# Handing two 512 KB round trips through memory from the sync queue to ScalarE's queue

## The chip, the cores and the metric

One core of a Trainium2 chip runs the whole kernel. The metric is the device time of one execution in microseconds (us); the time that is quoted is the median of several executions.

## What is computed

One layer of a hybrid encoder on 256 tokens of width 2048, in float32. Cut to what matters here:

```
u = rmsnorm(x) @ W_in
x = x + concat(fox_attention(u), ssd(u)) @ W_out          # the "output" groups o0..o3
g, up = split(rmsnorm(x) @ W_gate_up)
x = x + (silu(causal_dwconv3(g)) * up) @ W_down           # the "down" groups, 0..3
x = x + sigmoid(rmsnorm(x) @ W_ple_gate) * (p @ W_ple_proj)
out = rmsnorm(x)
```

## The kernel before

**Chunks.** Every product with a weight is made by streaming the weight in chunks of 128 x 1024 float32 (512 KB). A chunk is loaded by the sync queue (SP) into one of four slots of `w_raw`, split by ScalarE (ACT) into `w_hi` (`make_hi`, L349) and by VectorE (DVE) into the rest, `w_lo` (`make_lo`, L354), and used by TensorE (PE) in 12 matmuls, high times high, high times low and low times high. Four chunks are in the ring: the load of chunk n waits for `w_lo` of chunk n-4, and `make_hi` of chunk n waits until PE has used chunk n-4. So when ACT makes chunk 3 of a section, PE has just ended the last chunk of the section before.

**The turning.** The residual x lies in `xtok` with tokens on the partitions. The next product needs it with features on the partitions, split into a high and a low part (`hHi`, `hLo`, both in the tile `h_parts`). For each group of 512 output columns this is done in steps:
- DVE adds the group's PSUM banks to `xtok` (`add_columns`, L1499) and transposes blocks of 32 x 32 into `turn_blocks` (L1538).
- `carry_out` (L460): one DMA of 512 KB writes these blocks to `turn_dram` in HBM.
- `carry_back` (L471): when it has landed, four DMAs of 128 KB read them back in pieces of 512 bytes into `turned_cols`, with features on the partitions.
- `turn_out` or `turn_down`: ACT makes four tiles of 128 x 256 of the high part (L1128), DVE four of the low part (L1489).

ACT meanwhile squares the new columns (`square_columns`, L1146) and, when the group is the last of its product, takes the root for the norm (`root_x`, L1155). The norm's factor is applied later, so that nothing here waits for it but the root itself.

**The order.** Each engine runs its instructions in the order in which they are written, and that order is set by hand: the number k (or n) of the chunk behind which a step stands. `LEAD` is 3 and `KU` is 8. A section "gate_up, first half" has 8 chunks, and chunk k of it multiplies features 2k and 2k+1 (blocks of 128), so that chunk 6 is the first that needs the blocks 12 and 13 of the last output group o3. In the last section ("tail") the first gate group has the order gate chunks 0 to 5, one chunk of `W_ple_proj` (place 6), gate chunks 6 and 7: the blocks 12 and 13 of the last down group are needed at place 7.

The last group of each product stands apart from the others: its `carry_out` is written behind place `LAST_OUT` of the chunks that follow and its `carry_back` behind `LAST_BACK`; `LAST_H` = 8 is the place at which ACT and DVE make the blocks. A queue that runs the step first waits: `carry_out` for `blocks_made` and for the landing of the group before, `carry_back` for the landing of the write (`blocks_out`) and for `h_lo_made`, which says that `turned_cols` has been read for the group before.

Of the kernel before, what the change touches and what calls it, by code (L numbers as in the profile page):

```python
# [46 lines left out]
def build(nc, x, p, mix_norm_w, w_in, fox_forget_bias, ssd_conv_w, ssd_conv_b, ssd_dt_bias, ssd_A_log,  # L47
          ssd_D, ssd_norm_w, w_out, ffn_norm_w, w_gate_up, ffn_conv_w, ffn_conv_b, w_down, ple_norm_w,
          w_ple_gate, w_ple_proj, final_norm_w, out):
    _, T, D = x.shape  # L50
    TT = T // P
    KD = D // P
# [17 lines left out]
    KU = KD // 2  # L70
# [34 lines left out]
    NDN = D // COLS  # L105
# [23 lines left out]
    with ctx:  # L129
# [189 lines left out]
        def load_chunk(sp, n, src, q=0):  # L319
            if n >= RING:  # L320
                sp.wait_ge(w_lo_made, n + RING * q - RING + 1)
            sp.dma_start(w_raw[:, n % RING, :].rearrange("p (a c) -> p a c", a=src.shape[1]), src).then_inc(w_landed[n % RING], 16)

        def load_unit_chunk(sp, n, src, q=0):
            if n >= RING:
                sp.wait_ge(w_lo_made, n + RING * q - RING + 1)
            for a in range(2):
                sp.dma_start(w_raw[:, n % RING, a * COLS:(a + 1) * COLS].rearrange("p (b c) -> p b c", b=2),
                             src[:, a, :, :]).then_inc(w_landed[n % RING], 16)
# [13 lines left out]
        def make_hi(act, n, q=0):  # L343
            act.wait_ge(*landed(n, q))
            if RING <= n < n_last:
                act.wait_ge(w_used, n + RING * q - RING + 1)
            elif n >= n_last + KP - 1:
                act.wait_ge(w_used, n_last)
            act.activation(parts(n)[0], w_raw[:, n % RING, :], ACT.Copy).then_inc(w_hi_made, 1)  # L349
# [6 lines left out]
        def chunk_of(g, c):  # L356
            return g.view[:, 2 * c:2 * c + 2, g.col:g.col + COLS]
# [88 lines left out]
        def carried_before(norm, i):  # L446
            return NDN * (norm - 1) + i
# [6 lines left out]
        def carry_out(sp, norm, i):  # L454

            n = carried_before(norm, i)
            sp.wait_ge(blocks_made, TT * (n + 1))
            if n > 0:
                sp.wait_ge(cols_landed, 64 * n)
            sp.dma_start(turn_dram.rearrange("t p c -> p t c"), turn_blocks[norm - 1][:, :, :]).then_inc(blocks_out, 16)  # L460

        def carry_back(sp, norm, i):

            n = carried_before(norm, i)
            sp.wait_ge(blocks_out, 16 * (n + 1))
            if i > 0:
                sp.wait_ge(h_lo_made, norm * KD + MT * i)
            by_quarter = turn_dram.rearrange("t (i k) (j c) -> j k (t i) c", k=BLK, j=NB)
            for j in range(NB):
                rows_ = slice(j * BLK, (j + 1) * BLK)  # L470
                sp.dma_start(turned_cols[norm - 1][rows_, :, :, :].rearrange("p a m q -> p a (m q)"),  # L471
                             by_quarter[j]).then_inc(cols_landed, 16)
# [47 lines left out]

        LEAD = 3
        CARRY_OUT, CARRY_BACK, H_AFTER = LEAD + 5, LEAD + 7, LEAD + 7
        LAST_OUT, LAST_BACK, LAST_H = LEAD + 5, LEAD + 6, LEAD + 5
        assert LAST_H == KU
        GROUP_OUT, GROUP_BACK, GROUP_READY, Z0_LATER = LEAD + 5, LEAD + 6, LEAD + 6, 3
        end = {g.name: done[g.name] for g in in_groups + out_groups}
# [94 lines left out]
        def run(table, n, steps):  # L621
            for name, args in table.get(n, ()):
                if name in steps:
                    steps[name](*args)
# [15 lines left out]
        def _(sp):  # L640
# [44 lines left out]
            for j in range(2):  # L685
                for k in range(KU):
                    run(sp_before, n_ffn + j * KU + k, steps)
                    if j * KU + k == LAST_OUT:
                        carry_out(sp, 1, NDN - 1)
                    if j * KU + k == LAST_BACK:  # L690
                        carry_back(sp, 1, NDN - 1)
                    load_unit_chunk(sp, n_ffn + j * KU + k, gu[:, 2 * k:2 * k + 2, :, j * 2 * P:(j + 1) * 2 * P])
            with sp.Fori(0, NU // 2 - 1) as i:
                for j in range(2):
# [26 lines left out]
                    for j in range(RING):  # L721
                        load_chunk(sp, n0 + peeled + j, wdn_v[:, bass.ds(q * (2 * RING) + 2 * (peeled + j), 2), cols], q)
            for i, (g, c) in enumerate(tail):
                if i == LAST_OUT:
                    carry_out(sp, 2, NDN - 1)
                if i == LAST_BACK:
                    carry_back(sp, 2, NDN - 1)
                load_chunk(sp, n_ple + i, chunk_of(g, c))
                if i == RING:

                    sp.dma_start(gain_fin[:, :], final_norm_w.rearrange("(a n) -> a n", a=1).to_broadcast([P, D])).then_inc(gain_fin_landed, 16)
# [394 lines left out]
        def _(act):  # L1126
# [22 lines left out]
            def root_x(norm):  # L1149
                if norm == 0:  # L1150
                    act.wait_ge(x_squared, TT)
                    act.wait_ge(tables_loaded, 1)
                else:
                    act.wait_ge(x_summed, norm)
                act.activation(root[:, :], x_sum[:, norm, :], ACT.Sqrt, bias=eps[:, :], scale=1.0 / D).then_inc(root_made, 1)  # L1155
# [136 lines left out]
            def leave_out(i):  # L1292
                square_columns(1, i)

            def turn_out(i):
                for k in range(MT * i, MT * (i + 1)):
                    make_h(1, k, par_ffn)

            def leave_down(g):
                square_columns(2, g)  # L1300

            def turn_down(g):
                for k in range(MT * g, MT * (g + 1)):
                    make_h(2, k, par_ple)
# [27 lines left out]
            def unit_leave(u, half, unit_end):  # L1332

                act.wait_ge(w_used, unit_end)
                act.wait_ge(rms_col_made, 2)
                if not (isinstance(u, int) and u == 0):
                    act.wait_ge(unit_turned, u * TT)
                for t in range(TT):
                    copy(unit_tok[:, t, :], ps[:, UNIT_BANKS[half][t], :], rms_col[:, t:t + 1]).then_inc(unit_left, 1)
# [18 lines left out]
            for j in range(2):  # L1358
                for k in range(KU):
                    make_hi(act, n_ffn + j * KU + k)  # L1360
                    if j == 0:
                        run(act_after, n_ffn + k, steps)
                        if k == LEAD:
                            leave_out(NDN - 1)
                        if k == LEAD + 1:
                            root_x(1)
                    else:
                        if k == 0:
                            turn_out(NDN - 1)
                        if k == U_LEAVE:  # L1370
                            unit_leave(0, 0, n_ffn + KU)
# [27 lines left out]
            def ple_sigmoid(i, only=(0, 1)):  # L1399
                for t in only:  # L1400
                    if t == 0:
                        act.wait_ge(gate_first, i + 1)
                        act.wait_ge(rms_col_made, 3)
                    else:
                        act.wait_ge(w_used, n_ple + GROUP * (i + 1) if i < NDN - 1 else n_last + 1)
                    if i > 0:
                        act.wait_ge(ple_mul, TT * (i - 1) + t + 1)
                    act.activation(pg_sig[:, t, :], ps[:, GATE_BANKS[i % 2][t], :], ACT.Sigmoid,
                                   scale=rms_col[:, t:t + 1]).then_inc(ple_sig, 1)

            def square(i, t):
                act.wait_ge(out_added, TT * i + t + 1)
                if i + t > 0:
                    act.wait_ge(out_squared, TT * i + t)
                act.activation(squares[:, :], xtok[:, t, i * COLS:(i + 1) * COLS], ACT.Square,
                               accum_out=out_ssq[:, t, i:i + 1]).then_inc(out_squared, 1)

            for n in range(len(tail)):
                make_hi(act, n_ple + n)
                if n == LEAD:  # L1420
                    leave_down(NDN - 1)
                if n == LEAD + 1:
                    root_x(2)
                if n == LAST_H:
                    turn_down(NDN - 1)
                for i in range(NDN - 1):
                    if n == i * GROUP + SIG_AT:
                        ple_sigmoid(i)
                    if n == i * GROUP + SQUARE_AT:
                        for t in range(TT):  # L1430
                            square(i, t)
# [576 lines left out]
```

## Time and profile before

| | |
|---|---|
| time, median of 3 runs | 1205.61 us (1204.74 to 1206.5) |
| the profiled execution's own time | 1207.3 us |
| its span | 1205.4 us |
| TensorE busy | 1192.6 us, 99% of the span |
| VectorE busy | 794.1 us |
| ScalarE busy | 674.1 us |
| mean granted clock of TensorE | 0.998 of full speed |

The span runs from the first to the last instruction of the profiled execution; the 1.9 us between it and that execution's time lie around it. All places in the trace are in us from the span's start. A busy PE is an engine with a matmul in it.

### The profile page before, as it was taken

How to read it: one execution, taken by the hardware profiler on the slowest of the kernel's cores; microseconds unless marked ns; L12 is line 12 of the kernel's file. 1: busy time of each engine (PE TensorE's matmuls, PEld its weight loads, DVE VectorE, ACT ScalarE, POOL GpSimd, SP SyncE). 2: the span in 40 equal slices, each digit the busy share in tenths (PEclk: the TensorE clock that was granted, in tenths of full speed). 3: DMA queues.
4: the chain of work that ended last, by engine and by line, in shares of the span. 5: the costliest groups of instructions: out<-in, count | busy, mean ns of one | idle time of the engine just before them, and what ended most of it. 6: DMA issues, size and time to landing. Idle time of an engine off the chain costs nothing.

```text
span 1205.4 us, 16744 instructions
## 1 busy us (share of the span) xinstructions
PE 1192.6 (99%) x5444; PEld 987.6 (82%) x5444; DVE 794.1 (66%) x1211; ACT 674.1 (56%) x901; POOL 35.3 (3%) x55
## 2 busy tenths in 40 slices
PE   9999999999999999999999999999999999999997
PEld 6888888888888788888888888888888888888886
DVE  5688787886667576766766767667655555555655
ACT  6555787676546555555645655555444444445555
POOL 3210110000100000000000000000000000000000
PEclk9999999999999999999999999999999999999999
DMA  8767996449677877777787787877867676767662
GB/s 276 219 200 241 282 279 191 125 136 261 204 229 248 258 235 244 239 246 241 228 252 242 238 248 229 249 246 231 246 205 220 204 224 198 216 210 248 206 193 105
DMA packets 227511, 270.96 MB, mean 225 GB/s; under 512 B 23136, under 2 KB 152388, under 8 KB 227332
## 3 DMA queue, kind: packets, MB, share of 16 engines
q1 hardware_dynamic: 225972, 266.57, 71.2%
q0 software_dynamic: 1312, 3.47, 1.0%
q8 instruction: 29, 0.48, 0.2%
q10 hardware_dynamic: 176, 0.27, 0.1%
q14 instruction: 22, 0.18, 0.0%
HBM read 247.66 MB, written 22.59 MB: 224 GB/s over the span
## 4 chain that ended last, share of the span: by engine, by line
PE 97%; DMA 1%; ACT 1%; DVE 0%; issue 0%; SPq 0%; ACTq 0%
PE ps L1054 13%; PE ps L1055 13%; PE ps L1056 13%; PE ps L485 11%; PE ps L487 11%; PE ps L486 11%; PE ps L1091 7%; PE ps L1089 7%; PE ps L1090 7%; PE ps L365 2%; DMA turn_dram<-turn_blocks 1%; PE ps L983 1%; PE ps L998 0%; PE ps L961 0%; PE ps L948 0%; PE ps L857 0%
## 5 line engine op out<-in xcount | busy, mean ns | idle before, releaser
L354 DVE TENSOR_TENSOR w_lo<-w_raw,w_hi 128x1024 fp32r<-128x1024 f32 x412 | 502.4, 1222 | 344.4 <-ACT w_hi L349 343.3
L349 ACT ACTIVATE w_hi<-w_raw 128x1024 fp32r<-128x1024 f32 x412 | 434.8, 1058 | 418.3 <-PE ps L1056 201.9
L1054 PE MATMUL ps<-w_hi,h_parts 128*128 128x512 f32 x704 | 274.0, 389 | 2.3 <-DVE h_parts L1489 2.3
L1055 PE MATMUL ps<-w_lo,h_parts 128*128 128x512 f32 x704 | 273.9, 389 | 0.0
L1056 PE MATMUL ps<-w_hi,h_parts 128*128 128x512 f32 x704 | 273.9, 389 | 0.0
L485 PE MATMUL ps<-w_hi,h_parts 128*128 128x512 f32 (+1 forms) x428 | 170.0, 397 | 0.0
L487 PE MATMUL ps<-w_hi,h_parts 128*128 128x512 f32 (+1 forms) x428 | 166.1, 388 | 0.0
L486 PE MATMUL ps<-w_lo,h_parts 128*128 128x512 f32 (+1 forms) x428 | 166.0, 388 | 0.0
L1054 PEld LDWEIGHTS ps<-w_hi,h_parts 128*128 128x128 f32 x704 | 132.2, 188 | 30.3 <-DVE h_parts L1489 2.7
L1056 PEld LDWEIGHTS ps<-w_hi,h_parts 128*128 128x128 f32 x704 | 132.2, 188 | 27.3
L1055 PEld LDWEIGHTS ps<-w_lo,h_parts 128*128 128x128 f32 x704 | 132.2, 188 | 27.3
L1089 PE MATMUL ps<-w_hi,act_parts 128*128 128x512 f32 x352 | 136.9, 389 | 0.0
L1090 PE MATMUL ps<-w_lo,act_parts 128*128 128x512 f32 x352 | 136.9, 389 | 0.0
L1091 PE MATMUL ps<-w_hi,act_parts 128*128 128x512 f32 x352 | 136.9, 389 | 0.0
L487 PEld LDWEIGHTS ps<-w_hi,h_parts 128*128 128x128 f32 x428 | 80.4, 188 | 17.0
L485 PEld LDWEIGHTS ps<-w_hi,h_parts 128*128 128x128 f32 x428 | 80.4, 188 | 15.6
L486 PEld LDWEIGHTS ps<-w_lo,h_parts 128*128 128x128 f32 x428 | 80.5, 188 | 15.4
L1090 PEld LDWEIGHTS ps<-w_lo,act_parts 128*128 128x128 f32 x352 | 66.1, 188 | 13.8
L1091 PEld LDWEIGHTS ps<-w_hi,act_parts 128*128 128x128 f32 x352 | 66.1, 188 | 13.8
L1089 PEld LDWEIGHTS ps<-w_hi,act_parts 128*128 128x128 f32 x352 | 66.1, 188 | 13.5
L485 PE MATMUL ps<-w_hi,mixHi 128*128 128x512 f32 x128 | 50.0, 391 | 0.0
L487 PE MATMUL ps<-w_hi,mixLo 128*128 128x512 f32 x128 | 49.8, 389 | 0.0
(243 smaller groups left out, 1001.2 us busy)
## 6 DMA issues: line engine op xcount, KB each, us to landing
w_raw<-in_w_gate_up SPq DMA_DIRECT2D x352, 256.0 KB, 3.5
w_raw<-in_w_down SPq DMA_DIRECT2D x88, 512.0 KB, 4.3
w_raw<-in_w_in SPq DMA_DIRECT2D x87, 512.0 KB, 4.5
w_raw<-in_w_out SPq DMA_DIRECT2D x32, 512.0 KB, 4.6
w_raw<-in_w_ple_gate SPq DMA_DIRECT2D x32, 512.0 KB, 4.3
unit_cols<-unit_dram SPq DMA_DIRECT2D x88, 128.0 KB, 2.9
unit_dram<-first_blocks SPq DMA_DIRECT2D x22, 256.0 KB, 3.2
unit_dram<-unit_spare SPq DMA_DIRECT2D x22, 256.0 KB, 3.4
```

Of the source, the lines that this page charges most:

```text
L349: act.activation(parts(n)[0], w_raw[:, n % RING, :], ACT.Copy).then_inc(w_hi_made, 1)
L354: dve.tensor_tensor(lo, w_raw[:, n % RING, :], hi, ALU.subtract).then_inc(w_lo_made, 1)
L365: mm = pe.matmul(ps[:, banks[t], :], h_part[:, k, t * P:(t + 1) * P], parts_[:, n % RING, kk * COLS:(kk + 1) * COLS], start=k == 0 and par ...
L485: pe.matmul(dst, a, hi, start=first and kk == 0, stop=False)
L486: pe.matmul(dst, a, lo, start=False, stop=False)
L487: mm = pe.matmul(dst, b, hi, start=False, stop=last and kk == 1)
L1054: pe.matmul(dst, a, hi, start=first and kk == 0, stop=False)
L1055: pe.matmul(dst, a, lo, start=False, stop=False)
L1056: mm = pe.matmul(dst, b, hi, start=False, stop=last and kk == 1)
L1089: pe.matmul(dst, a, hi, start=first and kk == 0, stop=False)
L1090: pe.matmul(dst, a, lo, start=False, stop=False)
L1091: mm = pe.matmul(dst, b, hi, start=False, stop=last and kk == 1)
```

## The change

Both DMA steps of the last output group and of the last down group are taken out of SP's program and written into ACT's, at new places. On SP a place stands ahead of the load of that chunk; on ACT it stands behind `make_hi` of that chunk. In both ACT programs the place `LAST_OUT` falls right behind `root_x`.

```
-        LAST_OUT, LAST_BACK, LAST_H = LEAD + 5, LEAD + 6, LEAD + 5
+        LAST_OUT, LAST_BACK, LAST_H = LEAD + 1, LEAD + 3, LEAD + 5
...
                     run(sp_before, n_ffn + j * KU + k, steps)
-                    if j * KU + k == LAST_OUT:
-                        carry_out(sp, 1, NDN - 1)
-                    if j * KU + k == LAST_BACK:
-                        carry_back(sp, 1, NDN - 1)
                     load_unit_chunk(sp, n_ffn + j * KU + k, gu[:, 2 * k:2 * k + 2, :, j * 2 * P:(j + 1) * 2 * P])
...
             for i, (g, c) in enumerate(tail):
-                if i == LAST_OUT:
-                    carry_out(sp, 2, NDN - 1)
-                if i == LAST_BACK:
-                    carry_back(sp, 2, NDN - 1)
                 load_chunk(sp, n_ple + i, chunk_of(g, c))
...
                         if k == LEAD + 1:
                             root_x(1)
+                        if k == LAST_OUT:
+                            carry_out(act, 1, NDN - 1)
+                        if k == LAST_BACK:
+                            carry_back(act, 1, NDN - 1)
...
                 if n == LEAD + 1:
                     root_x(2)
+                if n == LAST_OUT:
+                    carry_out(act, 2, NDN - 1)
+                if n == LAST_BACK:
+                    carry_back(act, 2, NDN - 1)
```

The sync queue at the start of gate_up, before and then after. Two gate_up loads make one chunk. The first `turned_cols` row is the group o2, the second is o3.

```order
L471 DMA turned_cols_88<-turn_dram 32x8x128 x4
L328 DMA w_raw<-in_w_gate_up 128x2x256 x6
L460 DMA turn_dram<-turn_blocks_87 128x2x512
L328 DMA w_raw<-in_w_gate_up 128x2x256 x2
L471 DMA turned_cols_88<-turn_dram 32x8x128 x4
L328 DMA w_raw<-in_w_gate_up 128x2x256 x14
L693 UNCONDITIONAL_BRANCH
```

```order
L471 DMA turned_cols_88<-turn_dram 32x8x128 x4
L328 DMA w_raw<-in_w_gate_up 128x2x256 x22
L689 UNCONDITIONAL_BRANCH
```

The five DMAs of o3 have left the queue: nothing stands between the loads of chunks 5 to 15 any more.

ScalarE at the start of the tail, before and then after; the one row `w_hi` between the squares (`unit_tok,x_ssq`) and the root is chunk 4.

```order
L1146 ACTIVATE unit_tok,x_ssq<-xtok 128x512 x2
L349 ACTIVATE w_hi<-w_raw 128x1024
L1155 ACT_TABLE_LOAD
L1155 ACTIVATE root<-x_sum,eps 128x2
L349 ACTIVATE w_hi<-w_raw 128x1024 x4
L1128 ACTIVATE h_parts<-turned_cols_90,par 128x256 x4
```

```order
L1138 ACTIVATE unit_tok,x_ssq<-xtok 128x512 x2
L349 ACTIVATE w_hi<-w_raw 128x1024
L1147 ACT_TABLE_LOAD
L1147 ACTIVATE root<-x_sum,eps 128x2
L460 DMA turn_dram<-turn_blocks_89 128x2x512
L349 ACTIVATE w_hi<-w_raw 128x1024 x2
L471 DMA turned_cols_90<-turn_dram 32x8x128 x4
```

The write stands behind the root and ahead of chunk 5, the four reads stand behind chunk 6 and ahead of chunks 7 and 8 and of the making of the blocks. At the start of gate_up ScalarE's rows read the same way, with the four tiles of group o2 between chunks 5 and 6.

## Rows read from the trace of the kernel before

**Rows 1.** The page, part 1: busy time and share of each engine.
```profile
PE 1192.6 (99%) x5444; PEld 987.6 (82%) x5444; DVE 794.1 (66%) x1211; ACT 674.1 (56%) x901; POOL 35.3 (3%) x55
```

**Rows 2.** Waits of TensorE: us in total, times, longest.
```profile
PE ps L1054 <- DVE h_parts L1489: 2.3, 1, 2.3
PE ps L839 <- DVE idle_in L1775: 1.3, 1, 1.3
PE ps L845 <- DMA mix_rows<-in_mix_norm_w: 0.7, 1, 0.7
```

**Rows 3.** Chain that ended last, 377 to 398: start, us, what.
```profile
381.56 1.31 DVE turn_blocks L1538 x2
382.87 0.02 issue
382.88 7.92 DMA turn_dram<-turn_blocks
390.80 0.02 issue
390.82 0.31 SPq L471
...
392.16 2.58 DMA turned_cols<-turn_dram
394.73 0.02 issue
394.76 0.03 ACT h_parts L1128
...
395.70 0.89 DVE h_parts L1489 x2
396.59 0.04 issue
396.63 0.50 PE ps L1054
```

**Rows 4.** Landings of the three earlier writes of turn_blocks (348.0, 359.2, 370.3).
```profile
DMA to landing us min/median/max: 3.1/3.1/3.1
...
DMA to landing us min/median/max: 5.0/5.0/5.0
...
DMA to landing us min/median/max: 5.9/5.9/5.9
```

**Rows 5.** ScalarE in order of time, 384 to 393.
```profile
384.94 0.29 ACT L1155 ACTIVATE root<-x_sum,eps 128x2 f32<-128x2 f32 x1 [1.36 <-DVE x_sum L1512]
385.14 1.04 ACT L349 ACTIVATE w_hi<-w_raw 128x1024 fp32r<-128x1024 f32 x1
...
387.69 1.04 ACT L349 ACTIVATE w_hi<-w_raw 128x1024 fp32r<-128x1024 f32 x1
...
392.08 1.06 ACT L349 ACTIVATE w_hi<-w_raw 128x1024 fp32r<-128x1024 f32 x1 [1.45 <-DMA w_raw<-in_w_gate_up]
```

**Rows 6.** The store that ScalarE's queue issues at the end.
```profile
L1479 ACTq DMA_DIRECT2D out_x<-xtok x1: 367/367/367, 1201.4 to 1201.4; - x1
```

**Rows 7.** VectorE in order of time: the low parts of group o2.
```profile
387.36 1.67 DVE L1489 SCALAR_TENSOR_TENSOR h_parts<-turned_cols,par,h_parts 128x256 fp32r<-128x256 f32 x4
```

**Rows 8.** Sync queue in order of time, 384 to 393.
```profile
384.86 1.21 SPq L328 DMA_DIRECT2D w_raw<-in_w_gate_up  x2
390.82 1.79 SPq L471 DMA_DIRECT2D turned_cols<-turn_dram  x4
```

**Rows 9.** DMA issues, 385.43 to 385.46: the second load of chunk 8.
```profile
w_raw<-in_w_gate_up SPq DMA_DIRECT2D x1, 256.0 KB, 6.6
```

**Rows 10.** Busy time by stretch; the last two columns are DMA share and GB/s.
```profile
384.00:388.00 4.00, 4.00 (x19) 3.34 (x18) 2.85 (x6) 3.06 (x7) 0.00 (x0) 1.00 0.95 324
388.00:392.00 4.00, 4.00 (x20) 3.30 (x19) 3.38 (x5) 1.79 (x2) 0.00 (x0) 1.00 0.22 75
```

**Rows 11.** ScalarE in the tail, in order of time.
```profile
1105.59 0.29 ACT L1155 ACTIVATE root<-x_sum,eps 128x2 f32<-128x2 f32 x1
1105.79 2.21 ACT L349 ACTIVATE w_hi<-w_raw 128x1024 fp32r<-128x1024 f32 x2
...
1113.35 1.69 ACT L1128 ACTIVATE h_parts<-turned_cols,par 128x256 fp32r<-128x256 f32 x4
```

**Rows 12.** Sync queue in the tail, in order of time.
```profile
1103.53 0.37 SPq L460 DMA_DIRECT2D turn_dram<-turn_blocks  x1
...
1106.87 1.81 SPq L471 DMA_DIRECT2D turned_cols<-turn_dram  x4
```

**Rows 13.** DMA issues of the tail: the write at 1103.53; the fourth read, at 1108.2.
```profile
turn_dram<-turn_blocks SPq DMA_DIRECT2D x1, 512.0 KB, 3.3
...
turned_cols<-turn_dram SPq DMA_DIRECT2D x1, 128.0 KB, 4.4
```

**Rows 14.** TensorE in the tail: first matmul of place 7.
```profile
1117.56 0.39 PE L485 MATMUL ps<-w_hi,h_parts 128*128 128x512 f32 x1
```

## The prediction

> **What bounds the kernel now.** The page's busy times come first: TensorE is busy 1192.6 us, 99% of the span [rows 1]. So the change can only be worth what TensorE waits for, and the view of waits says how much that is: 2.3 us once for `h_parts`, and else only waits in the first microseconds [rows 2]. The third view, the chain that ended last, shows that the 2.3 us belong to the very step that is moved. From 382.88 the chain leaves the engines: the write of o3's blocks takes 7.92 us to land, the four reads are issued at 390.82, the last one at 392.16 lands 2.58 us later, ACT makes two tiles from 394.76, DVE ends their low parts at 396.59, TensorE resumes at 396.63 [rows 3]. With no wait it would have resumed at 396.63 - 2.3 = 394.3. The same step in the tail is not on the chain: ACT makes the blocks from 1113.35, 1.87 us later (as 394.76 to 396.63) they could be used at 1115.2, and place 7 starts at 1117.56 [rows 11, 14]. It has 2.3 us to spare.
>
> Why is the write slow? The same 512 KB took 3.1, 5.0, 5.9 and then 7.92 us in the four output groups [rows 3, 4], and 3.3 us in the tail [rows 13]. From 384 to 388 the DMA engines are 0.95 busy [rows 10]: the write stands in SP's queue behind six loads of 256 KB. So its price is mostly a backlog, not the transfer.
>
> **The change, start of gate_up.** Nothing is computed less; the five DMAs only get other start times. I follow them in order.
>
> The write. Now it is issued when the blocks are made, 382.88. After the change ACT issues it behind the root, which ends at 384.94 + 0.29 = 385.23 [rows 5]: 2.35 us later. A DMA issued by ACT costs it 0.37 us [rows 6].
>
> How long it then takes on the other queue no row shows. From below 3.1 us, the calm write [rows 4]. From above: in the kernel before, everything that is posted by 385.44 (the loads of chunks 5 to 7, this write and chunk 8) has landed when the second load of chunk 8 has, 385.44 + 6.6 = 392.04 [rows 9]; a write that came last of all would land there, 6.8 us after its issue. I take 4.6, the middle of the calm tail's 3.3 and o2's 5.9, since its own queue is empty but the engines are not: it lands at 389.85.
>
> The row says that in one queue a backlog costs this write up to 7.92 - 3.1 = 4.8 us. The Trainium skill, DMA: Bandwidth & Descriptors, "Queues, rings and completion order", says that a DMA engine takes turns between the queues for which it has work; by it the write would pass the backlog at about half rate, close to my 4.6. The same page, "Issuing engines are not separate DMA queues", says that issuing from several engines saves only the time of issuing. By that sentence the write would come out near the upper bound, 392.04, and it speaks against this change. No row here has a busy SP queue and an ACT queue side by side, so both stay open.
>
> The reads. ACT reaches them behind chunk 6. Its `make_hi` starts at 387.69 for 1.04 us [rows 5]; with the issue ahead of it (0.37) that ends at 389.1. It also waits for o2's low parts, which end at 387.36 + 1.67 = 389.03 and shift by as much: 389.4 [rows 7]. So the reads begin at B = the later of 389.45 and the landing; by my value 389.85, against 390.82 before. The gain in B is 0.97 us, and never over 1.37.
>
> What is queued behind them. The four issues take 1.79 us on SP [rows 8]; that is now ACT's time. `make_hi` of chunks 7 and 8 follow, one in about 1.0 us: chunk 8 ends at B + 3.8. DVE follows with 1.2 us each and ends `w_lo` of chunk 8 at B + 5.3, then the two low parts, 0.89 [rows 3]: TensorE could not resume before B + 6.1. Before, SP issued them and ACT did chunk 7 meanwhile. The other bound is the landing: before, the last read landed 394.74 - 390.82 = 3.92 us after the first was issued [rows 3]. But then the DMA engines were only 0.22 busy [rows 10], since SP itself, waiting for the write, held back the loads of chunks 9 and 10. After the change these loads go out at about 387.5 and 390.5, and the reads meet the second. In the tail, beside loads, the last read landed 1108.2 + 4.4 - 1106.87 = 5.7 us after the first was issued [rows 12, 13]. I take 4.5, nearer to the row of the place itself, so TensorE resumes at B + 4.5 + 1.87 = B + 6.4, which is over the floor of B + 6.1.
>
> Sum: 389.85 + 6.4 = 396.25, against 396.63: 0.4 us gained. The corners: B = 389.45 and the floor of 6.1 give 395.55, 1.1 us gained; B = 392.04 and 5.7 + 1.87 = 7.6 give 399.6, 3.0 us lost.
>
> The loads that SP issues earlier are worth nothing: hi of chunk 8 did wait for its load until 392.08 [rows 5], but it is needed by TensorE two chunks after chunk 6, and the load moves little, since the same bytes are ahead of it.
>
> **The change, tail.** The root ends at 1105.88 instead of a write issued at 1103.53 [rows 11, 12]: 2.35 us later again, and ACT's order is the same. The write took 3.3 us here [rows 13] and the engines carry less, so B = 1109.2; chunks 5 and 6 end at 1105.79 + 2.21 + 0.37 = 1108.4 and hide under it. The reads land at 1109.2 + 5.7 = 1114.9, the blocks are ready 1.87 us later, 1116.8, and place 7 starts at 1117.56. Cost 0, covered by 0.8 us of gate and projection matmuls. It was 2.3 us, so most of this cover is used up: each microsecond by which the write takes longer than 4.1 comes out of TensorE's time.
>
> In all -0.4 us: 1207.3 - 0.4 = 1206.9 for an execution like the profiled one. The median of the runs is 1.7 us under the profiled one's time, so 1205.61 - 0.4 = 1205.2.
>
> **The rivals.**
> - A, the write doesn't pass the backlog and ACT stands in wait for it. For it: the loads of chunk 8, posted at that very time, took up to 6.6 us [rows 9]. Against it: another queue. ACT's chunks 7 and 8, the tiles and all of DVE hang behind it. B = 392.04 and reads beside loads give +3.0 us, 1208.6. It costs over 2.4 us from B = 391.5 on if the reads take 5.7 us, from 392.9 on if only the order of ACT and DVE counts. 1 in 10.
> - B, milder: write 5 to 6 us, reads 4.5 to 5.7. Break-even is B = 390.2, a write of 5.0 us. The stall grows by 0 to 2.4 us; in the middle +1.1, 1206.7. 18 in 100.
> - C, the cover in the tail is gone: a write of 5.9 us there gives B = 1111.8, blocks ready at 1119.4, a new wait of 1.8 us, 1207.0 with the gain of 0.4. Against it: the calm 3.3. With a bad start of gate_up it makes the run slower. 5 in 100.
> - D, the whole stall goes and more with it, over 2.4 us: 1203.2. Against it: ACT can't issue the reads before 389.45, so 1.1 us is the most that this place gives. 4 in 100.
>
> **How the numbers follow.** The forecast, 0 to 1.1 us gained, has 63 in 100; its own range is 1204.3 to 1206.0. 0.2% is 2.4 us, about what a measurement of this kernel tells from no change. The forecast, B and half of C fall within it: 0.63 + 0.18 + 0.03 = 0.84; faster is D, 0.04; slower is A and the rest of C, 0.12. The three runs before lie 0.9 us to either side of their median, so the low end is 1205.61 - 1.1 - 0.7 = 1203.8, and the high end reaches into A, 1208.0.
>
> **What would show it.** Of the changed kernel: the write issued by ACT's queue at about 385.3, landing near 389.9 (4 to 5 us); the reads issued by ACT within half a microsecond of that; TensorE's wait for `h_parts` between 1.2 and 2.3 us and still the only one past the start; ACT's `make_hi` of chunk 7 about 2 us later than before; in the tail no wait of TensorE. I am wrong if the write lands after 391 (A, B), if the reads take over 5 us from the first issue, if a wait stands at 1117, or if TensorE's wait is under 1.2 us, which would say that ACT's order is no floor.

## The result, and the profile after

The changed kernel takes 1212.93 us (median of 6 runs, 1211.65 to 1215.11), the kernel before 1205.5 us (6 runs, 1204.74 to 1207.57). The ratio is 1.0059 with a 95% interval of 1.0049 to 1.0068: 7.4 us slower. The prediction was 1205.2 us, in a range of 1203.8 to 1208.0. In the runs of this document two executions fell into a much slower state, one of e4 (2137.47 us) and one of the kernel before beside e8 and e10 (1719.88 us); no ratio contains them, the medians as given do.

The profiled execution of the changed kernel took 1211.92 us, with a span of 1210.2 us, 4.8 us over the span before. In the order of the prediction, first the waits of TensorE (us in total, times, longest us):

```profile
PE ps L1046 <- DVE h_parts L1489: 4.0, 1, 4.0
PE ps L485 <- DVE h_parts L1489: 1.6, 1, 1.6
PE ps L831 <- DVE idle_in L1775: 1.3, 1, 1.3
```

The wait at gate_up is 4.0 us and not 2.3 [rows 2], and there is a new one of 1.6 us, L485, in the tail. Together 3.3 us more. The rest shows only in the busy time by stretch; its columns are those of [rows 10], and the number after POOL is the granted clock:

```profile
392.00:396.00 4.00, 0.66 (x3) 0.20 (x2) 1.69 (x3) 1.22 (x4) 0.00 (x0) 1.00 1.03 302
396.00:402.00 6.00, 5.34 (x13) 4.18 (x14) 2.62 (x5) 1.44 (x3) 0.00 (x0) 0.50 0.51 161
402.00:404.00 2.00, 2.00 (x9) 1.58 (x8) 0.67 (x1) 1.06 (x1) 0.00 (x0) 0.79 0.02 7
```

TensorE had been idle since 392.66. From 396 to 402 its granted clock is 0.50, the lower of its two levels (1.2 and not 2.4 GHz), and 0.79 as the mean of 402 to 404 is another 0.84 us of it: 6.8 us in all. The chain that ended last shows the same, and the path to it (start us, us, what):

```profile
383.26 4.73 DMA turn_dram<-turn_blocks
388.01 0.34 ACTq L471
...
389.38 5.38 DMA turned_cols<-turn_dram
...
396.66 0.79 PE ps L1046
397.45 0.43 PE ps L1047
397.88 0.43 PE ps L1048
...
403.23 0.23 PE ps L1046
```

A matmul starts every 0.43 us and not every 0.23 us. TensorE works from 396.66 to 403.0 at this speed. The 14 matmuls of this stretch take 6.3 us; at 0.50 us for the first [rows 3] and 0.23 for the others they would take 3.4 to 3.5: 2.9 us lost, nearly as much as both waits together have grown. After the wait of 2.3 us in the kernel before, the granted clock stays at 1.00.

To compare times: in this execution all of this part of the program ran 1.7 us earlier than in the one of [rows 3] (`make_hi` of chunk 3 starts at 376.39 and not 378.13), for reasons ahead of it. Shifted by 1.7, the write is issued at 385.0, it lands at 389.7, and the reads begin at 389.7. The prediction had 385.2, 389.85 and 389.85. Up to there it held. Then the last read lands not 4.5 but 5.38 + 389.38 - 388.01 = 6.75 us after the first was issued. ScalarE in order of time:

```profile
383.26 0.41 ACTq L460 DMA_DIRECT2D turn_dram<-turn_blocks  x1
...
388.01 1.85 ACTq L471 DMA_DIRECT2D turned_cols<-turn_dram  x4
389.96 2.01 ACT L349 ACTIVATE w_hi<-w_raw 128x1024 fp32r<-128x1024 f32 x2 [2.58 <-PE ps L1048]
394.78 1.70 ACT L1120 ACTIVATE h_parts<-turned_cols,par 128x256 fp32r<-128x256 f32 x4 [2.81 <-DMA turned_cols<-turn_dram]
```

ScalarE's order is no bound here: it has made chunks 7 and 8 by 391.97 and then stands 2.81 us for the reads. The 2.58 us that the view puts down to TensorE are something else: ScalarE stands there until the write has landed at 387.99 and then issues the reads until 389.86. In e6 below, where it has no reads to issue, it makes chunk 7 right behind chunk 6. In the tail the same rows are:

```profile
1108.58 0.40 ACTq L460 DMA_DIRECT2D turn_dram<-turn_blocks  x1
...
1114.29 1.82 ACTq L471 DMA_DIRECT2D turned_cols<-turn_dram  x4
...
1120.37 1.70 ACT L1120 ACTIVATE h_parts<-turned_cols,par 128x256 fp32r<-128x256 f32 x4 [2.14 <-DMA turned_cols<-turn_dram]
```

The write landed 5.7 us after its issue (3.3 before [rows 13]), the reads 6.1 us after theirs. And the sync queue, which waits for nothing of o3 any more, issues loads without a break through the whole place:

```profile
376.76 32.18 SPq L328 DMA_DIRECT2D w_raw<-in_w_gate_up  x22
```

So the account from the two traces is: +1.7 us of wait at gate_up, +2.9 us of slow clock behind it, +1.6 us of wait in the tail: 6.2 us. The spans differ by 4.8 us, and by 6.5 with the 1.7 us by which this execution came to the place earlier, so all but 0.3 us of the profiled execution is accounted for. The medians differ by 7.4 us. The theory: it is the loads of chunks 9 and 10, no longer held back by the sync queue's own wait, that make the reads late. The rivals: ScalarE's queue is slow by itself; or the late start of the write is what costs.

### The profile page after: what moved, and what is told of

It reads as the page before. It is cut to its first block, busy times and chain, and to the rows that moved or that the text cites. A ratio compares the mean times of both kernels' runs of the same rounds, so it can differ in the third digit from the quotient of the medians.

```text
span 1210.2 us, 16744 instructions
## 1 busy us (share of the span) xinstructions
PE 1194.8 (99%) x5444; PEld 988.8 (82%) x5444; DVE 793.8 (66%) x1211; ACT 673.6 (56%) x901; POOL 35.3 (3%) x55
## 4 chain that ended last, share of the span: by engine, by line
PE 97%; DMA 1%; ACT 1%; DVE 0%; issue 0%; ACTq 0%
PE ps L1046 13%; PE ps L1047 13%; PE ps L1048 13%; PE ps L485 11%; PE ps L487 11%; PE ps L486 11%; PE ps L1083 7%; PE ps L1082 7%; PE ps L1081 7%; PE ps L365 2%; PE ps L975 1%; PE ps L990 0%; PE ps L953 0%; DMA turned_cols<-turn_dram 0%; PE ps L940 0%; DMA turn_dram<-turn_blocks 0%
## 5 line engine op out<-in xcount | busy, mean ns | idle before, releaser
L485 PE MATMUL ps<-w_hi,h_parts 128*128 128x512 f32 (+1 forms) x428 | 170.2, 398 | 1.6 <-DVE h_parts L1489 1.6
L485 PEld LDWEIGHTS ps<-w_hi,h_parts 128*128 128x128 f32 x428 | 80.4, 188 | 17.5 <-DVE h_parts L1489 2.0
L485 PE MATMUL ps<-w_hi,mixHi 128*128 128x512 f32 x128 | 50.0, 391 | 0.0
```

The lines of the kernel that those rows point to most:

```text
L485: pe.matmul(dst, a, hi, start=first and kk == 0, stop=False)
```

## The experiments

Each was compared with the kernel before in runs on the same chip, whose median was 1205.3 to 1205.8 us. The profiled executions come to the start of gate_up at different times, for reasons ahead of it. So where two of them are compared, times are counted from the start of `make_hi` of chunk 3 there, called C: 378.13 in the kernel before, 376.39 in the changed one.

### The two places apart

The first kernel (e1) leaves only gate_up on ScalarE's queue, the second (e2) only the tail; the other place is that of the kernel before.

The first against the changed kernel (the second does the same for the other place):

```
             for i, (g, c) in enumerate(tail):
+                if i == LEAD + 5:
+                    carry_out(sp, 2, NDN - 1)
+                if i == LEAD + 6:
+                    carry_back(sp, 2, NDN - 1)
                 load_chunk(sp, n_ple + i, chunk_of(g, c))
...
                 if n == LEAD + 1:
                     root_x(2)
-                if n == LAST_OUT:
-                    carry_out(act, 2, NDN - 1)
-                if n == LAST_BACK:
-                    carry_back(act, 2, NDN - 1)
```

> Only the turning of the last output group (start of gate_up) is on ScalarE's queue; the last down group stays with the sync queue. The account from the two traces: the wait of TensorE there grows from 2.3 to 4.0 us (+1.7) and after it TensorE's granted clock is 0.50 for 6.8 us (+3.4), so this half alone should cost about 5.1 us of the 7.4: 1210.6 us. Rival, the clock has nothing to do with the move and the cost is that of the waits alone: +1.7 us, 1207.2. Rival, the cost lies mostly in the tail: under +1 us.

Measured: 1210.84 us, ratio 1.0047 (1.003 to 1.0064), 5.5 us. The wait of TensorE in it:

```profile
PE ps L1050 <- DVE h_parts L1489: 3.8, 1, 3.8
```

And the stretch of it and the one behind it, with the clock ahead of the last two columns:

```profile
394.00:398.00 4.00, 0.22 (x2) 0.05 (x1) 1.87 (x4) 1.92 (x5) 0.00 (x0) 1.00 0.90 280
398.00:402.00 4.00, 4.00 (x11) 3.14 (x12) 1.92 (x3) 0.73 (x1) 0.00 (x0) 0.57 0.31 90
```

This half alone costs far more than its added wait, and the clock is down again: a mean of 0.57 over 4 us is 3.4 us at 0.50, half of what was expected.

> Only the turning of the last down group (tail) is on ScalarE's queue. By the account: one wait of TensorE of 1.6 us in the tail, no stretch at clock 0.50, 1207.1 us. Rival, the tail is where most of the cost lies: over +4 us, 1209.5 or more.

Measured: 1208.93 us (10 runs), ratio 1.0025 (1.0015 to 1.0035), 3.6 us and so 1.8 more than expected. Its rows say why. The wait of TensorE in the tail, and that at gate_up, where this kernel is the one before:

```profile
PE ps L485 <- DVE h_parts L1489: 2.0, 1, 2.0
...
PE ps L1050 <- DVE h_parts L1489: 0.6, 1, 0.6
```

Here too the clock falls, as the stretches around the end of the wait show:

```profile
1117.00:1119.00 2.00, 1.16 (x4) 0.97 (x5) 1.93 (x5) 2.00 (x4) 0.00 (x0) 0.88 0.64 237
1119.00:1123.00 4.00, 4.00 (x13) 3.13 (x13) 2.01 (x2) 1.02 (x2) 0.00 (x0) 0.63 0.39 137
```

In the ten runs the times fall into two groups, 1206.8 to 1207.4 us (mean granted clock 0.998 to 0.999) and 1208.8 to 1210.4 us (0.996 to 0.998). The profiled execution, 1209.2 us, has the slow stretch and is of the upper group. That the others of this group have it too, and that the wait is the steady part of the cost, is read from the mean clocks and not shown.

The second row matters for e1 too: if the kernel before mostly waits 0.6 us at gate_up and not 2.3, the wait of e1 is 3.2 us longer, and with 1.6 us for its slow stretch (an estimate: 3.4 us at 0.43 us a matmul instead of 0.23) that is 4.8 of the 5.5 us. By the same count the changed kernel loses 3.4 + 2.9 + 1.6 = 7.9 us, where the medians differ by 7.4.

### The clock

The changed kernel with work in the wait (e3):

```
+                        if k == 6:
+                            pe.wait_ge(x_new, TT * NDN)
+                            for i in range(30):
+                                pe.matmul(ps[:, SET_D[0], 0:T], hHi[:, 0, 0:P], hHi[:, 1, :], start=True, stop=True)
                         pe.wait_ge(h_lo_made, KD + 2 * k + 2)
```

> The changed kernel with 30 more matmuls of 256 columns on TensorE, into a bank that nobody reads, between chunks 5 and 6 of gate_up: about 3.4 us of work inside a wait of 4.0 us. Their results are not used. If the idle time is what brings the clock down, the granted clock stays at 1.00 there and the time falls by the 3.4 us, to 1209.5, though work was added. Rival, the drop of the clock does not come from the idle time: the clock still falls and the time stays at 1212.9 or rises.

Measured: 1211.49 us (4 runs), ratio 1.0054 (1.0037 to 1.0071). The granted clock stayed at 1.00 through the place and behind it:

```profile
392.00:398.00 6.00, 4.74 (x35) 4.40 (x34) 3.08 (x6) 2.64 (x5) 0.00 (x0) 1.00 0.89 261
398.00:404.00 6.00, 6.00 (x28) 4.93 (x27) 2.45 (x2) 2.00 (x3) 0.00 (x0) 1.00 0.29 88
```

The mean granted clock of its runs is 0.997 to 0.999, against 0.995 to 0.997 for the changed kernel, which speaks for the idle time as what brings the clock down. The time fell by 1.4 us and not 3.4, and by its interval even that is not certain. In the profile TensorE still waits 1.3 us behind the added matmuls: the last read landed 7.5 us after the first was issued instead of 6.75, so that TensorE resumed 21.2 us after C and not 20.3. From C to the end of the span it is 831.7 us, against 833.8 in the changed kernel. The 2.1 us gained and the 0.9 us of later start come to 3.0, close to the 2.9 us put down to the slow stretch. The mechanism is borne out, in one profiled execution; its worth is not shown by the medians.

### The loads beside the reads

The changed kernel, with the sync queue waiting for the reads ahead of the load of chunk 9, at both places (e4):

```
+                    if j * KU + k == 9:
+                        sp.wait_ge(cols_landed, 64 * (carried_before(1, NDN - 1) + 1))
...
+                if i == 9:
+                    sp.wait_ge(cols_landed, 64 * (carried_before(2, NDN - 1) + 1))
```

> The changed kernel, and the sync queue waits ahead of the load of chunk 9 until the reads have landed, at both places, so that the loads of chunks 9 and later do not run beside the reads. If the loads beside them make the reads late, the last read lands about 4 us after the first issue (6.75 and 6.1 us now), TensorE's wait at gate_up falls to about 1.6 us with the clock at 1.00, the tail's wait of 1.6 us goes, and the time is 1205 us. Rival, reads from ScalarE's queue are slow by themselves: they still land over 6 us after the first issue, and the time stays at 1212 us or more.

Measured: 1207.46 us (10 runs), ratio 1.0016 (1.0006 to 1.0026). ScalarE's queue still issues the reads, and its rows now are:

```profile
387.87 1.84 ACTq L471 DMA_DIRECT2D turned_cols<-turn_dram  x4
...
391.83 1.71 ACT L1124 ACTIVATE h_parts<-turned_cols,par 128x256 fp32r<-128x256 f32 x4
...
1108.71 1.82 ACTq L471 DMA_DIRECT2D turned_cols<-turn_dram  x4
...
1112.65 1.71 ACT L1124 ACTIVATE h_parts<-turned_cols,par 128x256 fp32r<-128x256 f32 x4
```

The tiles start 3.96 and 3.94 us after the reads, instead of 6.77 and 6.08, and meanwhile the DMA engines are half idle, 0.47 in the last but one column:

```profile
388.00:392.00 4.00, 4.00 (x19) 3.28 (x19) 1.75 (x2) 2.18 (x3) 0.00 (x0) 1.00 0.47 141
```

In the changed kernel the same column had 0.96 while the reads ran:

```profile
388.00:394.00 6.00, 4.66 (x21) 3.53 (x19) 3.17 (x3) 2.01 (x2) 0.00 (x0) 1.00 0.96 271
```

With the hold TensorE waits 1.6 us at gate_up and not in the tail. 5.5 of the 7.4 us are back, with a wait added and nothing else. The profiled execution (1204.61 us) is the fastest of its runs, but it came to the place early: from C to its end it takes 826.7 us, and e8 below, with the order of the kernel before at this place but for one load, 825.6. So about 1 us of the 2 that remain is in it, the wait of 1.6 us in place of 0.6. The rest isn't; the slower executions have a mean clock of 0.997 to 0.998.

The chain of e4 shows what ends this wait. It is no longer the reads:

```profile
389.83 1.05 ACT w_hi L349
...
390.91 2.36 DVE w_lo L354 x2
393.27 0.80 DVE h_parts L1493 x2
...
394.11 0.50 PE ps L1050
```

ScalarE could make chunk 7 only behind its four issues, and VectorE makes the low parts of chunks 7 and 8 ahead of those of the blocks. TensorE resumes 6.2 us after the first read is issued. With the reads on the sync queue it is 5.8 us (the kernel before, e6, e8).

### Write and reads apart

Four kernels that divide the change differently. e6 has only the writes on ScalarE, e7 only the reads, e5 has both, with the write behind the squares and ahead of the root, and e9 has both on the sync queue, one place later than before.

e6 against the changed kernel, in the tail (gate_up and e7 read the same way, with `carry_out` at `LEAD + 5` for e7):

```
+                if i == LEAD + 6:
+                    carry_back(sp, 2, NDN - 1)
                 load_chunk(sp, n_ple + i, chunk_of(g, c))
...
-                if n == LAST_BACK:
-                    carry_back(act, 2, NDN - 1)
```

e5 against the changed kernel, on ScalarE:

```
                 if n == LEAD:
                     leave_down(NDN - 1)
+                    carry_out(act, 2, NDN - 1)
                 if n == LEAD + 1:
                     root_x(2)
-                if n == LAST_OUT:
-                    carry_out(act, 2, NDN - 1)
```

e9 against the kernel before:

```
-        LAST_OUT, LAST_BACK, LAST_H = LEAD + 5, LEAD + 6, LEAD + 5
+        LAST_OUT, LAST_BACK, LAST_H = LEAD + 6, LEAD + 7, LEAD + 5
```

> Only the two writes are on ScalarE's queue, behind the root; the reads stay with the sync queue at their old place ahead of chunk 9, so that the sync queue again holds the loads of chunk 9 and later back until the write has landed. If it is the loads beside the reads that cost the time, the reads land about 4 us after the first issue at both places, TensorE waits 1.5 to 2.3 us at gate_up and not at all in the tail, 1205 us. Rival, the write's late start or ScalarE's queue costs by itself: 1207.5 us or more.

Measured: 1205.98 us (10 runs), ratio 1.0001 (0.9991 to 1.0011). The writes start as late and take as long as in the changed kernel, as the issue at gate_up shows (KB, us to landing):

```profile
turn_dram<-turn_blocks ACTq DMA_DIRECT2D x1, 512.0 KB, 4.8
```

But TensorE waits only once past the start, and for less than in [rows 2]:

```profile
PE ps L1050 <- DVE h_parts L1489: 1.2, 1, 1.2
```

> Only the reads are on ScalarE's queue, behind chunk 6; the writes stay with the sync queue at their old place. The loads of chunk 9 and later run beside the reads. By the account: at gate_up the reads land 6.75 us after the first issue, TensorE waits 4 to 5 us and its clock falls to 0.50 for 3.4 to 6.8 us; in the tail the write is early again and nothing waits; 1210 us. Rival, the write's late start is what costs: then this kernel is at 1206 us.

Measured: 1210.7 us (4 runs), ratio 1.005 (1.0033 to 1.0066). The tiles at gate_up start 6.3 us after the reads, in the tail 8.4 us, where the early write leaves just enough cover. ScalarE at gate_up:

```profile
390.02 1.88 ACTq L471 DMA_DIRECT2D turned_cols<-turn_dram  x4
396.30 1.70 ACT L1124 ACTIVATE h_parts<-turned_cols,par 128x256 fp32r<-128x256 f32 x4 [2.28 <-DMA turned_cols<-turn_dram]
```

And what TensorE waited for it:

```profile
PE ps L1050 <- DVE h_parts L1489: 3.2, 1, 3.2
```

The clock stayed up in this one profiled execution (the fastest of the four, mean clock 0.998) and was 0.996 to 0.997 in the others.

> The changed kernel with both writes issued by ScalarE right behind the squares, ahead of chunk 4 and of the root, 2.3 us earlier and so ahead of the load of chunk 8 again. The reads stay on ScalarE's queue behind chunk 6. By the account the write lands early enough that the reads start as soon as ScalarE is there; at gate_up they still run beside the loads of chunks 9 and 10, with a wait of 4 us and the slow clock, but the tail's wait goes: 1210.6 us. Rival, the lateness of the write is the cause at both places: 1205.5 us.

Measured: 1210.48 us (4 runs), ratio 1.005 (1.0033 to 1.0067). TensorE waits 3.3 us at gate_up with a slow stretch behind it (and 0.3 us once more ahead of it), and not in the tail. An early write alone does not help gate_up: it took 6.1 us to land.

> The kernel before with both steps on the sync queue as they were, one place later: the write behind the load of chunk 8, the reads behind the load of chunk 9. Nothing is on ScalarE's queue. If the order against the loads is the cause and not the queue, the write at gate_up lands near 392 to 393, TensorE waits 3 to 5 us there with the clock at 0.50 for some microseconds, the tail loses 0 to 2 us: 1208 to 1211 us. Rival, ScalarE's queue is the cause: 1205.5 us.

Measured: 1208.46 us (9 runs), ratio 1.003 (1.0016 to 1.0044). With nothing on ScalarE's queue, TensorE waits 3.2 us at gate_up. The sync queue there:

```profile
386.52 0.55 SPq L460 DMA_DIRECT2D turn_dram<-turn_blocks  x1
387.12 1.55 SPq L328 DMA_DIRECT2D w_raw<-in_w_gate_up  x2
390.74 1.79 SPq L471 DMA_DIRECT2D turned_cols<-turn_dram  x4
```

The load of chunk 9 now goes out ahead of the reads, the last of which lands 4.5 us after the first was issued, against 3.9. So loads beside the reads cost time on the sync queue as well. But this is the smaller part: the reads start 13.0 us after C, against 11.6 in e6, whose wait is 2 us shorter. The write, the reads and one chunk all moved in this kernel, so that it doesn't price them apart.

### The last gap, and what could be won

> The reads on ScalarE's queue behind chunk 6, the writes on the sync queue at their old place (1210.7 us in that form), and now the sync queue waits ahead of the load of chunk 9 until the reads have landed. If the loads beside the reads are the whole harm of moving the reads, the reads land within 4.5 us of the first issue, TensorE waits 1 to 2.5 us with the clock at 1.00 and the time is 1205.5 to 1206.5 us. Rival, ScalarE's standing in wait costs by itself: 1208 us or more.

This is e7 with the two waits of e4 (e12). Measured: 1205.83 us (10 runs), ratio 1.0005 (0.9995 to 1.0014). The same two waits took 1210.7 to 1205.8 us, with ScalarE's queue still issuing the reads at gate_up:

```profile
388.77 1.83 ACTq L471 DMA_DIRECT2D turned_cols<-turn_dram  x4
392.71 1.71 ACT L1128 ACTIVATE h_parts<-turned_cols,par 128x256 fp32r<-128x256 f32 x4
```

The rival, that ScalarE's standing in wait costs by itself, is out by its time. TensorE waits 1.1 us, and as in e4 it resumes 6.2 us after the first read is issued.

> The kernel before, and the sync queue waits ahead of the load of chunk 9 not only for the write but until the reads have landed. It prices the holding back itself. If it is free, 1205.4 us; and if loads beside the reads still cost the kernel before something, up to 0.5 us less. Rival, the loads that are held back another 4 us become late for TensorE and this explains what is left of the changed kernel with the loads held back (1207.5 us): 1207 us or more.

Measured: 1204.99 us (10 runs), ratio 1.0001 (0.999 to 1.0011). The load of chunk 9 goes out 4.0 us after the first read at gate_up instead of 1.8, and 5.2 instead of 1.9 in the tail: holding the loads back costs nothing that can be measured.

> Both writes issued by ScalarE right behind the squares, ahead of chunk 4 and the root; the reads stay with the sync queue at their old place ahead of chunk 9, which holds the loads of chunk 9 and later back. This takes from the change what passes the backlog and leaves what hurt. The write at gate_up starts when it did before and lands 1 to 3 us earlier, the reads start at about 389 and land 4 us later, TensorE waits 0.5 to 1 us instead of 0.6 to 2.3, the tail nothing: 0.5 to 1.5 us faster than before, 1204.7 us. Rival, the write's backlog was never worth anything in most executions: no difference.

Measured: 1205.84 us (11 runs), ratio 1.0002 (0.9993 to 1.0011): no difference, and so the rival. In this kernel (e10) the write was issued by ScalarE at 380.92, in an otherwise empty queue, and took 7.0 us to land:

```profile
turn_dram<-turn_blocks ACTq DMA_DIRECT2D x1, 512.0 KB, 7.0
```

> The kernel before with both writes one place earlier on the sync queue, ahead of the load of chunk 7 instead of behind it. The write is then behind two gate_up loads fewer, and the load of chunk 7 is issued 2.5 us later. If only the backlog of the write matters, it lands 1 to 2 us earlier and TensorE's wait shrinks by as much: 1204.5 us. Rival, the later load of chunk 7 makes ScalarE's chunk 7 and 8 late and takes it back: 1205.5 us or more.

This is the kernel before with `LAST_OUT` at `LEAD + 4` (e8). Measured: 1205.62 us (11 runs), ratio 0.9999 (0.999 to 1.0009): no difference. Its write and its reads at gate_up:

```profile
turn_dram<-turn_blocks SPq DMA_DIRECT2D x1, 512.0 KB, 4.1
...
388.67 1.79 SPq L471 DMA_DIRECT2D turned_cols<-turn_dram  x4
```

With two loads fewer ahead of it the write, issued at 382.45, lands in 4.1 us, at 386.6; in the kernel before and in e2 it took 7.9 and 5.9. But the reads go out 2.1 us later still, because `carry_back` also waits for `h_lo_made`, VectorE's low parts of group o2. They start 11.0 us after C in e8 and, with the later write, in e2. Neither outcome that was expected has this reason: no earlier write can bring the reads forward of that point, and the load of chunk 7 was not late.

In e2 and in e8 TensorE waited 0.6 us. The 2.3 us of [rows 2], where the reads start 12.7 us after C, belong to that execution, not to every one, and there was less to win than the prediction thought. No kernel tried here beats the one before.

## Why the prediction was wrong

- **What bounds the kernel**: right, with one thing unseen. TensorE's waits are what the change can touch. But a wait costs more than its length where the clock falls behind it, and the wait of 2.3 us was one execution's; e2 shows 0.6 us at the same place. The prediction saw that the profiled execution was 1.7 us over the median, which is the difference of the two waits, and took its gain off the median all the same. How often the kernel before waits 2.3 us, no run shows.
- **The write at gate_up**: the numbers are right, issued at 385.0 after the shift (predicted 385.2), landed in 4.73 us (4.6). The reason given for 4.6, that its own queue is empty, is not borne out. Issued at the old time, from ScalarE's empty queue, it took 6.1 and 7.0 us (e5, e10); issued late, from the sync queue, 4.2 (e9). What goes with the short time is the late start and not the queue, and that 4.6, the middle of two other writes, came out was luck.
- **The reads at gate_up**: this is the step that failed first. The prediction saw that the sync queue's wait had held back the loads of chunks 9 and 10 and that the reads would now meet them, and took 4.5 us from the first issue. It measured 6.75 us, over the 5.7 that it had as its upper end. e4 and e12 show the cause: the same reads from the same queue land in 3.9 us when the loads are held back. e6 shows that the late write on ScalarE's queue is free as long as the sync queue still stands in its wait. Two kernels with the loads free and the write early (e5, e7) cost 1.005, two with them held (e6, e12) 1.0001 and 1.0005. The failed term is the 4.5 us, taken near the 3.9 us of a place where the loads were held back, which the change itself removed.
- **The floor of ScalarE's and VectorE's order**, B + 6.1: right, but not reached in the changed kernel, where ScalarE had made chunks 7 and 8 2.8 us before the reads were there and TensorE resumed at B + 8.6. e4 and e12, with the reads in time, resume at B + 6.2. Rival A did not come: the write landed in 4.73 us.
- **The term that was missing**: the clock. No row of the trace before had shown a stretch at 0.50 behind a wait of 2.3 us, and the sum priced a longer wait by its length alone. In the profiled execution this was 2.9 us, nearly half of the whole loss. With the waits alone, 3.3 us, the result would have been 1208.8 us: still slower, and still outside.
- **The tail**: the step failed in the write. It was taken to land in the 3.3 us of [rows 13] since the engines carry less there. But behind the root it is issued at 1108.58, 0.14 us after the 512 KB load of chunk 8, which it used to precede by 2 us, and it took 5.7 us. Rival C had described this with a write of 5.9 us and a wait of 1.8, at 5 in 100. The cover was sized about right: a write 1.6 us over the 4.1 that it allowed made a wait of 1.6 us. e5 and e7, with the write ahead of that load, have no wait in the tail.
- **The two readings of the page.** The early writes of e10 and e5, alone in their queue, took 7.0 and 6.1 us, and those on the sync queue at the same place 5.1 to 7.9 (e7 and the kernel before; e8, with two loads fewer ahead, 4.1). So a queue of its own did not let the write pass the backlog. The Trainium skill, DMA: Bandwidth & Descriptors, "Issuing engines are not separate DMA queues", says that issuing from several engines saves only the time of issuing; the measurement agrees. The same page, "Queues, rings and completion order", says that each DMA engine takes turns between the queues that have work for it. These runs neither show nor contradict that; what the prediction drew from it, a write that passes the backlog, did not come.

## What to carry to other kernels

- A queue that stands in a wait also holds back everything behind it. Before moving the wait, ask what it was keeping away: here the sync queue's wait for the write cleared the DMA engines for the four reads that TensorE waits for. Moved, it has to be put back by hand.
- In these runs a second queue gave another order, not more room. Give it what nobody waits for, or hold the bulk loads while it runs.
- Where a wait of TensorE grows by microseconds, as here to between 2.0 and 4.0, price a slow stretch behind it as well (1.6 and 2.9 us here), as something that may or may not come. And a wait of one or two microseconds is to be taken from several executions.
- Ask for everything that a step waits for. The earlier write of e8 gave nothing, because the reads also waited for VectorE.

## What the runs showed of the hardware

TensorE's granted clock fell to 0.50 behind idle times of 4.0, 3.8, 3.3 and 3.2 us and once behind 2.0 us, but not behind one of 3.2 us (e7) and one of 2.3 us (before), nor behind any of 1.6 us or less. The slow stretch was 6.8 us long in the changed kernel and 3.4 us in e1, e2, e5 and e9. In it a matmul of 512 columns started every 0.43 us instead of every 0.23. The Trainium skill, TensorE: Matmul & The Clock Gate, "Part 1: The HAM clock gate", has the clock depend on how busy the engine has been recently; e3, where work in the idle time kept it up, agrees.

A write of 512 KB from SBUF to HBM took 3.0 to 3.6 us when issued ahead of a load of 512 KB and 5.2 to 5.7 us when issued within 0.5 us behind one (the changed kernel, e6, e9), on either queue, in the tail.

At gate_up the four reads had landed 3.9 us after the first was issued when the load of chunk 9 was issued behind them, on either queue (the kernel before, e4, e6, e12). With that load ahead of them it was 4.5 us (e9), and with the loads of chunks 9 and 10 ahead of or between them 6.25 to 7.5 us (e7, the changed kernel, e3). In the tail, with loads free to run beside them, it was 5.8 us and 6.8 us from the sync queue too (the kernel before, e8).

What stays open: which executions of a kernel with a wait of 2 to 3 us get the slow clock; how often the kernel before waits 2.3 us and not 0.6; and about 1 of the 2 us that e4 keeps over the kernel before.
